# The inner levels of a triangular inverse as full-array matmuls of 32 moving columns, and one Gram step one part later

## The reference, cut to what matters

```python
def _wkv_step(S, inp):
    r, w, k, v, kk, b = inp
    sa = jnp.einsum('bhvk,bhk->bhv', S, -kk)
    S = S * w[:, :, None, :] + sa[..., :, None] * b[:, :, None, :] + v[..., :, None] * k[:, :, None, :]
    y = jnp.einsum('bhvk,bhk->bhv', S, r)
    return S, y
```

## Time and profile before

| | |
|---|---|
| median of 3 runs | 1875.71 us (1875.41 to 1878.2) |
| profiled execution | 1879.94 us, its span 1878.2 us |
| TensorE (PE) busy | 1542.3 us, 82% of the span, mean granted clock 0.906 |
| VectorE (DVE) busy | 648.0 us, 35% |
| ScalarE (ACT) busy | 304.9 us, 16% |
| GpSimd (POOL) busy | 63.6 us, 3% |
| TensorE in 40 slices | 7 in the first, then 9 up to slice 21, after that 5 to 7 |
| DMA share in 40 slices | 7 in the first, 2 or 3 up to slice 17, 9 from slice 22 on (the last 5) |

### The profile page before, as it was taken

The page is one execution under the profiler, slowest core; times in us unless marked ns, Lnnn a source line. Parts: engine busy times, 40 slices in busy tenths (PEclk is TensorE's granted clock), DMA queues, the critical chain, the costliest instruction groups (busy, mean ns, idle before and its releaser), DMA issues.

```text
span 1878.2 us, 24556 instructions
## 1 busy us (share of the span) xinstructions
PE 1542.3 (82%) x8870; PEld 880.0 (47%) x8870; DVE 648.0 (35%) x1288; ACT 304.9 (16%) x704; POOL 63.6 (3%) x103
## 2 busy tenths in 40 slices
PE   7999999999999999999996675666757667576574
PEld 4676767676767676767752231222312223122121
DVE  6746565656565656410121120111201112010013
ACT  2323232323232323100112000000000000000012
POOL 1101010101010101000000000000000000000000
PEclk9999999999999999999997887888878888788787
DMA  7323232323232323374589999999999999999995
GB/s 286 109 100 113 92 120 82 120 82 120 82 120 82 120 82 120 110 292 165 204 373 426 429 426 429 429 428 428 429 428 427 429 429 429 427 429 430 428 403 212
DMA packets 71904, 510.35 MB, mean 272 GB/s; under 512 B 20496, under 2 KB 23696, under 8 KB 37808
## 3 DMA queue, kind: packets, MB, share of 16 engines
q1 hardware_dynamic: 71808, 509.60, 67.2%
q0 software_dynamic: 48, 0.12, 0.0%
HBM read 499.87 MB, written 9.82 MB: 271 GB/s over the span
## 4 chain that ended last, share of the span: by engine, by line
PE 41%; DMA 34%; DVE 16%; issue 4%; ACT 2%; SPq 1%; DVEq 1%; ACTq 0%
DMA arena<-w_up 22%; DVE arena L1424 16%; DMA arena<-w_down 12%; PE ps_PJ L723 11%; PE ps_C L1069 8%; PE ps_PJ L923 7%; ACT arena L1152 2%; SPq L560 1%; PE ps_C L1120 1%; PE ps_SB L1120 1%; PE ps_YB L1120 1%; PE ps_RT L1120 1%; PE ps_C L696 0%; PE ps_PJ L1023 0%; PE ps_SB L852 0%
## 5 line engine op out<-in xcount | busy, mean ns | idle before, releaser
L723 PE MATMUL ps_PJ<-arena 128*128 128x320 f32 x1792 | 536.6, 437 | 0.0
L1069 PE MATMUL ps_C<-arena 128*32 128x512 f32 x2048 | 285.1, 719 | 178.4 <-DMA arena<-w_gate 110.3
L723 PEld LDWEIGHTS ps_PJ<-arena 128*128 128x128 f32 x1792 | 324.7, 190 | 124.6 <-issue 17.9
L1424 DVE TENSOR_TENSOR arena<-arena,ps_PJ 128x512 f32<-128x512 f32 (+2 forms) x112 | 73.5, 657 | 614.7 <-PE ps_PJ L1023 495.3
L1069 PEld LDWEIGHTS ps_C<-arena 128*32 128x32 f32 x2048 | 79.3, 130 | 377.4 <-issue 375.0
L1152 ACT ACTIVATE arena<-arena 32x160 f32<-32x160 f32 (+9 forms) x350 | 146.6, 419 | 322.0 <-DVEq L422 134.7
L1424 DVE TENSOR_TENSOR arena<-arena 128x512 f32<-128x512 f32 (+12 forms) x311 | 161.8, 520 | 73.5 <-ACTq L422 41.2
L1152 ACT ACTIVATE arena<-ps_C 128x128 f32<-128x128 f32 (+3 forms) x68 | 27.4, 403 | 893.2 <-PE ps_C L1069 530.7
L923 PE MATMUL ps_PJ<-arena 128*128 128x320 f32 x512 | 142.4, 433 | 1.0 <-DVEq L422 1.0
L923 PEld LDWEIGHTS ps_PJ<-arena 128*128 128x128 f32 x512 | 95.5, 190 | 40.2 <-issue 3.3
L1424 DVE TENSOR_TENSOR arena<-ps_PJ,arena 128x512 f32<-128x512 f32 x32 | 22.1, 692 | 258.0 <-PE ps_PJ L1016 257.9
(11 more groups left out here) (181 smaller groups left out, 1175.7 us busy)
## 6 DMA issues: line engine op xcount, KB each, us to landing
arena<-w_down SPq DMA_DIRECT2D x64, 2048.0 KB, 21.5
arena<-w_gate SPq DMA_DIRECT2D x61, 2048.0 KB, 20.4
arena<-w_up SPq DMA_DIRECT2D x61, 2048.0 KB, 20.1
arena<-win SPq DMA_DIRECT2D x59, 1024.0 KB, 4.8
arena<-w_out SPq DMA_DIRECT2D x16, 1024.0 KB, 7.0
arena<-w_gate SPq DMA_DIRECT2D x6, 1024.0 KB, 8.0
arena<-xT SPq DMA_DIRECT2D x8, 640.0 KB, 7.4
arena<-s_ret SPq DMA_DIRECT2D x8, 512.0 KB, 3.8
```

The source lines that it names most:

```text
L723: last = mm(pj(j)[:, 0:T], wt[j % NSLOT][:, kt, :], hT[:, kt, :], start=kt == 0, stop=kt == KT - 1)
L1069: last = mm((GB, UB)[u][h * CAP:(h + 1) * CAP, :], xg[:, kt, h * CAP:(h + 1) * CAP], w[h](k), start=kt == 0, stop=kt == KT - 1)
L1424: ins = build(*args)
```

## The change

The inner levels 1 to 4 lose the narrow matmuls. `Ac` is spread once in u0 into `Ad`, a block-diagonal 128x128 matrix for each chunk. Step i is now four matmuls, one a chunk, with `Ad` stationary (128 columns) and the 32 columns of `Uc` moving; its result has the chunks side by side, and DVE multiplies it with the level's mask while it leaves PSUM (`Zp`, 128 elements). Step j has `Ud` stationary and `Zp` moving; DVE adds the result to `Uc`, transposes that in 32x32 squares into `Vc`, and spreads `Vc` into `Ud`. So step k (the transpose on TensorE with ACT's copy) and POOL's four masks go, and the masks are kept untransposed. Step i waits for `Uc` alone and step j for `Ud`. Level 5 stays, with k5 alone.

In `PLAN`, g4 moves from part 4 of tile v to part 5 (behind p2, still ahead of mu), rqb goes behind i3, and xv from behind ds2 to behind j3. `PLAN0` has the last two with it, since it takes tiles q to g from `PLAN`, and keeps g4. The bank C2 has six steps a pair instead of ten.

```diff
-    "C2": ["g2", "k1", "k2", "k3", "k4", "k5", "s0", "s1", "s2", "s3"],
+    "C2": ["g2", "k5", "s0", "s1", "s2", "s3"],
...
-    "v": "@r b2b cr -e3 | | | -my | g4 p2 | -mu g0 | g1 | g2 g3",
-    "q": "@v ax am -va u0 | cv us0 | | k1 i1 | zs1 xb | j1 pd | ds1 | k2 i2",
-    "kr": "@q | rqa j2 zs2 xk | | rqb k3 i3 | ds2 xv | j3 | | k4 i4",
+    "v": "@r b2b cr -e3 | | | -my | p2 | g4 -mu g0 | g1 | g2 g3",
+    "q": "@v ax am -va u0 | cv us0 | | i1 | zs1 xb | j1 pd | ds1 | i2",
+    "kr": "@q | rqa j2 zs2 xk | | i3 rqb | ds2 | j3 xv | | i4",
...
-        Zd = inv[:, 0:512].rearrange("p (b c j) -> p b c j", b=NB32, c=NC)
+        Ad = inv[:, 0:512].rearrange("p (c b j) -> p c b j", c=NC, b=NB32)
...
                 elif s[0] == "i":
...
+                    pe.wait_ge(inverse, NINV * p + 2 * int(s[1]))
                     for c in range(NC):
...
+                        last = mm(b[:, c * BK:(c + 1) * BK], Ad[:, c, :, :], Uc[:, c, :], start=True, stop=True)
+                    last.then_inc(full(s), 1)
...
                 elif s[0] == "j":
...
+                    wait_freed(pe, "i" + s[1], p)
+                    pe.wait_ge(inverse, NINV * p + 2 * int(s[1]) + 1)
+                    for c in range(NC):
+                        last = mm(b[:, c * BK:(c + 1) * BK], Ud[:, c, :, :], Zp[:, c, :], start=True, stop=True)
                     last.then_inc(full(s), 1)
...
-                elif s in ("k1", "k2", "k3", "k4"):
-                    wait_filled(act, s, p)
-                    A(V2[:, :, :], bank(s)[:, 0:P].rearrange("p (b j) -> p b j", b=NB32), ACT.Copy).then_inc(free(s), 1)
...
                 elif s == "u0":
                     dve.wait_ge(done("ac"), 2 * p + 1)
+                    spread(Ad, Ac).then_inc(inverse, 1)
                     TT(Vc[:, :, :], Ac[:, :, :], inner[0][:, None, :].broadcast_to([P, NC, BK]), ALU.mult)
                     TT(Vc[:, :, :], Vc[:, :, :], unit[:, None, :].broadcast_to([P, NC, BK]), ALU.add)
                     TR(Uc.rearrange("p c j -> p (c j)"), Vc.rearrange("p c j -> p (c j)")).then_inc(inverse, 1)
-                    spread(Ud, Uc).then_inc(inverse, 1)
+                    spread(Ud, Vc).then_inc(inverse, 1)
...
                 elif s in ("i1", "i2", "i3", "i4"):
                     wait_filled(dve, s, p)
-                    spread(Zd, bank(s)[:, 0:P].rearrange("p (b j) -> p b j", b=NB32)).then_inc(free(s), 1)
+                    TT(Zp[:, :, :], bank(s)[:, 0:P].rearrange("p (c j) -> p c j", c=NC),
+                       inner[int(s[1])][:, None, :].broadcast_to([P, NC, BK]), ALU.mult).then_inc(free(s), 1)
                 elif s in ("j1", "j2", "j3", "j4"):
                     wait_filled(dve, s, p)
                     TT(Uc[:, :, :], Uc[:, :, :], bank(s)[:, 0:P].rearrange("p (c j) -> p c j", c=NC), ALU.add).then_inc(free(s), 1).then_inc(inverse, 1)
-                    spread(Ud, Uc).then_inc(inverse, 1)
+                    if s == "j4":
+                        spread(Ud, Uc).then_inc(inverse, 1)
+                        return
+                    TR(Vc.rearrange("p c j -> p (c j)"), Uc.rearrange("p c j -> p (c j)"))
+                    spread(Ud, Vc).then_inc(inverse, 1)
...
-                    pool.wait_ge(done("ac"), 2 * p + 1)
-                    for k in range(1, INNER):
-                        TT(Am[:, k - 1, :, :], Ac[:, :, :], inner[k][:, None, :].broadcast_to([P, NC, BK]), ALU.mult).then_inc(lmk, 1)
```

More of the change, by code:

```diff
@@ L187, in cut @@
             return x.rearrange("p (c n) -> p c n", **axes) if axes else x
-        Zd = inv[:, 0:512].rearrange("p (b c j) -> p b c j", b=NB32, c=NC)
+        Ad = inv[:, 0:512].rearrange("p (c b j) -> p c b j", c=NC, b=NB32)
         Z5 = cut(512, 64, c=2)
-        Am = inv[:, 640:1152].rearrange("p (k c j) -> p k c j", k=INNER - 1, c=NC)
         Ac = cut(1152, 128, c=NC)
@@ L198, in build_program @@
         V = cut(2560, NCH * P, c=NCH)
-        V2 = cut(3200, 128, c=NB32)
+        Zp = cut(3200, 128, c=NC)
         V2d = inv[:, 3328:3584].rearrange("p (h c j) -> p h c j", h=2, c=NC)
@@ L356, in build_program @@
         vchain, achain, pchain = sem("vector_chain"), sem("scalar_chain"), sem("pool_chain")
+        NINV = 2 * INNER + 1
         N_TILE = {n: i for i, n in enumerate(TILES)}
@@ L761, in step @@
                     k = int(s[-1])
-                    pe.wait_ge(lmk, (INNER + 1) * p + k)
+                    pe.wait_ge(lmk, 2 * p + k)
                     if k == 1:
@@ L772, in step @@
                     mm(b[:, 0:P], V[:, NC, :], Zs, start=True, stop=True).then_inc(full(s), 1)
-                elif s[0] == "k":
-                    pe.wait_ge(inverse, 2 * (INNER * p + int(s[1])) - 1)
+                elif s == "k5":
+                    pe.wait_ge(inverse, NINV * p + 2 * INNER)
                     nc.tensor.transpose(b[:, 0:P], Uc[:, :, :], ident).then_inc(full(s), 1)
-                elif s[0] == "i":
[L777 to L782, removed]
-                    for c in range(NC):
-                        o = b[quarter[c], 0:P] if k < INNER else b[quarter[c], 0:HD]
-                        last = mm(o, Am[:, k - 1, c, :] if k < INNER else A5[:, c, :],
-                                  Ud[:, c, :, :] if k < INNER else Ud[:, c, 0:NB32:2, :], start=True, stop=True)
+                elif s == "i5":
+                    pe.wait_ge(inverse, NINV * p + 2 * INNER + 1)
+                    pe.wait_ge(done("ac"), 2 * p + 2)
+                    for c in range(NC):
+                        last = mm(b[quarter[c], 0:HD], A5[:, c, :], Ud[:, c, 0:NB32:2, :], start=True, stop=True)
+                    last.then_inc(full(s), 1)
+                elif s[0] == "i":
+                    pe.wait_ge(inverse, NINV * p + 2 * int(s[1]))
+                    for c in range(NC):
+                        last = mm(b[:, c * BK:(c + 1) * BK], Ad[:, c, :, :], Uc[:, c, :], start=True, stop=True)
+                    last.then_inc(full(s), 1)
+                elif s == "j5":
+                    wait_freed(pe, "i5", p)
+                    wait_freed(pe, "k5", p)
+                    for h in range(2):
+                        last = mm(b[quarter[2 * h], 0:P], Z5[:, h, :], V2d[:, h, :, :], start=True, stop=True)
@@ L1600, in step @@
                         RED(folded[:, k, :], whole(lvl[k]), AX_X, ALU.add)
-                    TR(packed[:, 0:INNER, :].rearrange("p k j -> p (k j)"), folded[:, 0:INNER, :].rearrange("p k j -> p (k j)"))
+                    TR(packed[:, 0, :], folded[:, 0, :])
+                    CP(packed[:, 1:INNER, :], folded[:, 1:INNER, :])
                     RED(unit, whole(ident), AX_X, ALU.add)
```

## The result

| | before | after |
|---|---|---|
| median | 1875.68 us (6 runs, 1875.41 to 1878.2) | 1892.96 us (6 runs, 1891.46 to 1893.77) |
| profiled execution, its span | 1879.94, 1878.2 us | 1893.29, 1891.1 us |
| one round of the pair loop | 92.82 us | 94.73 us |
| PE / DVE / ACT / POOL busy | 1542.3 / 648.0 / 304.9 / 63.6 us | 1556.7 / 648.6 / 296.2 / 45.8 us |

The ratio of the times is **1.0088, 95% interval 1.0075 to 1.0101**: slower by 0.9%, more than the 0.2% that can be told from no change. TensorE's busy time grew by 14.4 us and VectorE's by 0.6 us, for the spread of `Ad` and the new transposes make up for the shorter instructions at the i steps.

A forecast was written before the change was run, and what follows sets the result against it. TensorE bounds the kernel (busy 91.05 of 92.83 us a round). 0.60 + 2.11 - 1.23 + 0.12 = +1.6 us a round, 13.8 us in all, gave 1893.7 us, less 4.2: 1889.5 us; range 1873 to 1900.

The forecast's parts named there:

- A full-array block: Four matmuls with 128 stationary, 32 moving columns on TensorE: 0.11 us a record, 0.88 us a block.
- "0.05" behind it: Extra busy time of the four projection records behind a full-array block: 0.05 us of its 0.88.
- rival 1: Short matmuls run at the 0.06 us interval: a block costs 0.5 us, the kernel takes 1867 us; chance 0.18.
- TensorE's added work: From zs1 on in each round, longer i and j blocks and later zs2 and L831: +2.11 us.
- the 0.09 "ahead of a narrow block": Time lost on TensorE just before a narrow block, 0.09 us, part of its old price of 0.55.
- Waits at j3 and i4: TensorE's waits for VectorE at these two steps go wholly: -1.23 us a round.
- The walk of the two engines: TensorE and VectorE stepped on from zs1: Zp ready 1.8 us early for j3, Uc 1.1 us for i4.
- ScalarE's copies of k: Four copies that go with the transposes; nothing waited for them at j3 and i4, so no gain counted.
- zs1: Starts later behind spread(Ad) in u0, less 0.24 us back from POOL's lost mask: net +0.60 us a round.
- g4: L758 loses its 0.49 us wait, but mu then waits for VectorE's copy of y: 0, between 0 and -0.3.
- Register instructions: One more ahead of s2 and e3 on VectorE, in the chain to mu: 0.06 us each, +0.12 us.
- The sum: All terms together: +1.6 us a round, +2.6 us in the first pair, 13.8 us at the loop's end.

The follow-up runs named there:

- a_twice: The changed kernel with the four matmuls of step j4 issued twice: 1901.8 us, ratio 1.013.
- a_unmoved: The changed kernel with rqb and xv back in their old places: 1892.9 us, ratio 1.0094.
- b_moves: The kernel before with only the moves of rqb (behind i3) and xv (behind j3), none of the arithmetic: 1876.31 us, ratio 1.0002.
- a_us0: The changed kernel with us0 ahead of u0 on VectorE, and zs1 ahead of i1: 1888.1 us, ratio 1.0049.
- a_g4back: The changed kernel with the Gram product g4 (L758) back in its old part: 1892.01 us, ratio 1.0084.
- b_cr: The kernel before with cr's two copies moved behind mu's chain on VectorE: 1875.38 us, ratio 0.9995.
- b_three: The kernel before with rqb behind i3, xv behind k4, cr behind mu's chain, and g4 one part later: 1865.17 us, ratio 0.9936.

## Why the prediction was right, step by step

**A full-array block: right.** 0.11 us a record, as L851 showed, and 0.81 us to the next record for 0.83, since the first interval is 0.03 and not 0.06; `a_twice` confirms it by itself. Mis-sized was "0.05" behind it, taken from L881 and L882: the four records behind a block lose 0.08 us, so a block is 0.89, not 0.88.

Of the two sections of the Trainium skill's "TensorE: Matmul & The Clock Gate", the 25 ns of "Back-to-back issue gap", by which the time would have come out at rival 1 or below, fit only the first interval of a block (0.03 us) and none of the seven behind it. The weight load of "LDWEIGHTS (loading the stationary operand)", 107 ns for 128 columns, agrees with these intervals, 0.11 us each, though the records of the weight loads themselves last 0.19 us and overlap.

**TensorE's added work: 2.11 predicted, 2.28 found.** i2 to i4 cost 0.23 each, j1 and j3 0.34, 1.37 in all for 1.33. zs2 starts 0.81 us behind j2 and the projection 0.30 behind zs2, 0.34 more than before for 0.28. The largest miss is j4: L831 starts 0.91 us behind it (381.33 to 382.24), not 0.83, since its narrow matmuls have a gap of their own behind full-array ones. Before, where narrow followed narrow, it had none. I took off the 0.09 "ahead of a narrow block" at j4 and forgot that it now stands ahead of L831: 0.57 for 0.49.

**Waits at j3 and i4: right in size.** Both are gone, 1.23 us. But `a_unmoved` shows that they go without the moves of rqb and xv too, and at j3 without an earlier result from VectorE: the TensorE work that the prediction added in another term had filled the wait. The moves make `Zp` 1.6 us earlier still, and nothing uses it. The walk of the two engines had the right end and gave the moves a part that they don't have. I costed ScalarE's copies of k at nothing, since "nothing waited for them"; in the changed kernel they are gone, but `b_moves` shows that this held only by the place of xv: move it, and k4's copy is what TensorE waits for.

**zs1: +0.60 predicted, +0.71 found.** us0's transpose ends 0.61 us later against mu, as summed (the spread of `Ad`, less the 0.24 us that POOL's mask had cost). The rest is the way from there to zs1, 0.21 us for 0.11. What makes this 0.10 I haven't tested. `a_us0` shows the whole term to be avoidable, and more: +0.71 of the change against -0.83 of the order. In pair 0 zs1 came 0.86 us later.

**g4: right, at 0.** mu took the wait over, and `a_g4back` has mu at the same place. The limit of the statement is in `b_cr` and `b_three`: it holds as long as VectorE's copy of y ends as late as that.

**Register instructions: +0.12 predicted, +0.17 found** in the stretch from L831 to mu. VectorE's chain to the copy of y falls behind by 0.08 us at s2 and by 0.08 at e3, the two places where a register instruction was added. No run took these two out alone.

**The sum.** 0.71 + 2.28 - 1.23 + 0.17 = 1.93 a round, 1.91 measured. The three terms that missed all missed to the same side, 0.33 us together. With 3.0 for pair 0 the loop's end moves by 16.1 us instead of 13.8; the forecast of 1889.5 us lacks these 2.3 us and about one more behind the loop, where the executions differ by more than that.

## What to carry to other kernels

A wait that an engine shows is worth removing at the price of its own length at most, and first by order: here the waits of 1.23 us a round went at the price of 2.28 us of work on the engine that bounds the kernel, while moving two steps removed 0.98 of them without any. Price short full-array matmuls by the record and not by the moving columns: turning four narrow matmuls (32 stationary, 128 moving) into four with 128 stationary and 32 moving is the same number of multiplications, and took a block of 8 records from 0.36 to 0.81 us. Ahead of a step that two engines reach at nearly the same time, a move on either is worth only the difference between them, so such moves are tried together (b_cr 0.25 us a round, with g4 0.76).

## What the runs showed of the hardware that was not expected

- A second narrow block right behind a first costs 0.24 us, and one alone between full-array matmuls 0.55: more than half of a narrow block's price is paid at its two ends.
- A short group of full-array matmuls makes the four projection records behind it 0.08 us longer, in every block of the changed kernel; behind L881 and L882, with 64 moving columns, it is 0.05.
- A POOL instruction of 1.34 us that had started 0.44 us earlier held up one VectorE instruction of 0.29 us with two SBUF inputs by 0.76 us, so work moved from VectorE to POOL came back almost whole (0.14 us of 0.84 gained).
- Six copies queued on ScalarE (2.19 us) ahead of one that TensorE waits for cost TensorE 0.75 us at j4 (`b_moves`), on an engine that is busy for only 27 us of a round.
